# Two heads per attention step in the third block, and the delta-rule inverse in two 64-column tiles

## What is computed

```python
low = jnp.where(strict, jnp.einsum("bhnid,bhnjd->bhnij", kb, k) * decay, 0.0)
rhs = jnp.concatenate([v * beta, kb * jnp.exp(gc)[..., None]], axis=-1)
sol = lax.linalg.triangular_solve(low + jnp.eye(c, dtype=jnp.float32), rhs,
                                  left_side=True, lower=True, unit_diagonal=True)
```

```python
s = jnp.einsum('bhqd,bhkd->bhqk', qc, k) * scale
s = s + (cqc[..., None] - cum[:, :, None, :])
s = jnp.where(kpos[None, :] <= qpos[:, None], s, -jnp.inf)
p = jax.nn.softmax(s, axis=-1)
return jnp.einsum('bhqk,bhkd->bhqd', p, v)
```

## Time and profile before

| what | us |
|---|---|
| median of 3 runs (1081.12 to 1082.15) | 1081.33 |
| the profiled execution, its own time | 1081.43 |
| its span, first to last instruction | 1079.6 |
| PE busy | 1051.2 |
| DVE busy | 756.2 |
| ACT busy | 542.3 |
| PEld busy | 932.7 |

### The profile page before, as it was taken

How to read it: one execution, slowest core, us unless ns; L and a number is a source line. 1 busy time by engine, 2 the same in 40 slices (tenths; PEclk the granted TensorE clock), 3 DMA queues, 4 the chain that set the end, 5 groups by cost and what they waited for, 6 DMA issues and landing times.

```text
span 1079.6 us, 19214 instructions
## 1 busy us (share of the span) xinstructions
PE 1051.2 (97%) x7938; PEld 932.7 (86%) x7938; DVE 756.2 (70%) x1051; ACT 542.3 (50%) x601; POOL 12.6 (1%) x13
## 2 busy tenths in 40 slices
PE   9999999999999999999999999989999989999998
PEld 7999999999976798989899877659986659999986
DVE  6989947678458767677777856857797765556535
ACT  5675534563353463547536334576677654353331
POOL 0100000000000000000000000002000000000000
PEclk8999999999999999999999999999999999999999
DMA  8454432334325663425343354776344364545441
GB/s 343 157 180 155 157 118 90 138 125 159 115 79 213 252 239 155 132 104 193 121 157 118 118 200 153 310 291 260 127 156 156 103 243 163 195 172 181 176 163 51
DMA packets 26293, 181.32 MB, mean 168 GB/s; under 512 B 3040, under 2 KB 3296, under 8 KB 4960
## 3 DMA queue, kind: packets, MB, share of 16 engines
q1 hardware_dynamic: 25056, 174.66, 44.1%
q10 hardware_dynamic: 1152, 5.45, 1.2%
HBM read 179.04 MB, written 1.05 MB: 167 GB/s over the span
## 4 chain that ended last, share of the span: by engine, by line
PE 89%; DVE 7%; ACT 2%; issue 1%; DMA 1%; ACTq 0%; DVEq 0%; SPq 0%
PE PS L912 86%; DVE WL L1778 1%; PE PS L1065 1%; PE PS L1143 1%; DVE X L1972 1%; DVE X L1971 1%; DMA RAW<-wst 1%; PE PS L1289 0%; DVE layer_ln L2083 0%; DVE STAT L1953 0%; DVE X L1952 0%; ACT block L1606 0%; DVE X L2264 0%; DVE XTL L1995 0%; DVE layer L2076 0%
## 5 line engine op out<-in xcount | busy, mean ns | idle before, releaser
L912 PE MATMUL PS<-XTH,WH 128*128 128x256 f32 x1392 | 404.4, 291 | 0.7 <-issue 0.5
L912 PE MATMUL PS<-XTH,WL 128*128 128x256 f32 x1392 | 394.5, 283 | 0.0
L912 PE MATMUL PS<-XTL,WH 128*128 128x256 f32 x1392 | 394.4, 283 | 0.0
L1778 DVE TENSOR_TENSOR WL<-RAW,WH 128x2048 fp32r<-128x2048 f32 x138 | 316.9, 2297 | 107.9 <-ACT WH L1368 104.7
L1368 ACT ACTIVATE WH<-RAW 128x2048 fp32r<-128x2048 f32 x138 | 262.7, 1903 | 194.8 <-PE PS L912 191.2
L912 PEld LDWEIGHTS PS<-XTH,WH 128*128 128x128 f32 x1392 | 267.6, 192 | 6.3 <-issue 3.7
L912 PEld LDWEIGHTS PS<-XTL,WH 128*128 128x128 f32 x1392 | 267.7, 192 | 2.8 <-issue 2.6
L912 PEld LDWEIGHTS PS<-XTH,WL 128*128 128x128 f32 x1392 | 267.5, 192 | 0.0
L912 PE MATMUL PS<-WH,YH 128*128 128x512 f32 x224 | 89.6, 400 | 1.1 <-DVE YL L2256 1.1
L912 PE MATMUL PS<-WH,YL 128*128 128x512 f32 x224 | 87.4, 390 | 0.0
L912 PE MATMUL PS<-WL,YH 128*128 128x512 f32 x224 | 87.3, 390 | 0.0
(11 more groups left out here) (295 smaller groups left out, 1178.0 us busy)
## 6 DMA issues: line engine op xcount, KB each, us to landing
RAW<-wst SPq DMA_DIRECT2D x162, 1024.0 KB, 4.9
LNW<-lnrow ACTq DMA_DIRECT2D x3, 1024.0 KB, 6.4
RAW<-wst SPq DMA_DIRECT2D x4, 512.0 KB, 4.8
layer<-xt SPq DMA_DIRECT2D x2, 512.0 KB, 5.8
XR<-x ACTq DMA_DIRECT2D x1, 1024.0 KB, 6.2
out<-X SPq DMA_DIRECT2D x4, 256.0 KB, 2.1
CST<-cst ACTq DMA_DIRECT2D x1, 640.0 KB, 8.9
PT<-pt SPq DMA_DIRECT2D x1, 512.0 KB, 5.6
```

The lines of the kernel that those rows point to most:

```text
L912: return pe.matmul(o, lhsT, rhs, start=start, stop=stop)
L1778: tt(WL[:, i % RAW_RING, 0:n], RAW[:, i % RAW_RING, 0:n], as_float(WH[:, k % SPLIT_RING, 0:n]), ALU.subtract).then_inc(vector_done, 1)
```

## The change

The `gp` and `gu` matmuls of level 1 and above are each split in two, with 64 of the 128 weight columns and half of the output partitions each. Scores and value products of two heads become one PE step each (`scores:p`, `pvs:p`), in which the instructions of the two heads stand in turn. `scores:p` writes bank 0 and bank 1 and so claims both; it counts as read when DVE has done the odd head. `ORDER_T` is rewritten for the heads; `ORDER_V` and `ORDER_S` keep theirs but for `gm` ahead of `qn:1:1` ahead of `score:0` on DVE, and 14 ahead of 15.

```diff
@@ plan @@
         if n < HEADS:
-            step("score", n, on="TV" if FOX <= n < FOX + ML else "TVS", banks=(n % 2,), readers="V")
+            if n % 2 == 0:
+                step("scores", n // 2, on="T", banks=(0, 1), readers="V", read_in=("score", n + 1))
+            step("score", n, on="V" if FOX <= n < FOX + ML else "VS")
         if 1 <= n <= HEADS:
             step("turn", n - 1, on="TS", banks=(2,))
         if n >= 2:
-            if n % 2 == 0:
-                step("pv", n - 2, on="T", banks=(3,))
-            else:
-                step("pv", n - 2, on="TS" if FOX < n - 2 < FOX + ML else "TSV", banks=(3,), opens=False)
+            if n % 2:
+                ml = FOX < n - 2 < FOX + ML
+                step("pvs", n // 2 - 1, on="T", banks=(3,), readers="S" if ml else "SV", read_in=("pv", n - 2))
+                step("pv", n - 2, on="S" if ml else "SV")
@@ ORDER_T (one line of five) @@
-feat:4 first:feat:5 feat:5 grow:1 feat:6 first:feat:7 qn:1:0 feat:7 first:val:0:0 qn:1:1 score:0 val:0:0 first:val:0:1
+feat:4 first:feat:5 feat:5 grow:1 feat:6 first:feat:7 qn:1:0 feat:7 first:val:0:0 qn:1:1 scores:0 val:0:0 first:val:0:1 scores:1 turn:0 val:0:1 turn:1 first:val:1:0 scores:2 turn:2 pvs:0 turn:3
@@ ORDER_V @@
-split:94:114 feat:3 grow:0 split:96:116 feat:4 mod:1 grow:1 split:97:117 mb split:98:118 qn:1:0 gm score:0 qn:1:1
+split:94:114 feat:3 grow:0 split:96:116 feat:4 mod:1 grow:1 split:97:117 mb split:98:118 qn:1:0 gm qn:1:1 score:0
@@ t_gp, and t_gu alike with XI and PM @@
-                    last = mm(odd(PS[:, c, h * P:(h + 1) * P], i), DL[:, m, :], odd(U[:, m, :], i))
+                    for b in range(2):
+                        r = slice(b * HD, (b + 1) * HD)
+                        last = mm(odd(PS[r, c, h * P:(h + 1) * P], i), DL[:, m, r], odd(U[:, m, :], i))
@@ t_score becomes t_scores @@
-                o = PS[:, step.banks[0], :]
-                mm(o[:, 0:P], Q2[r:r + HD, q, 0:P], Q2[r:r + HD, k, 0:P])
-                mm(o[:, P:3 * P], Q2[r:r + HD, q, P:T], Q2[r:r + HD, k, :]).then_inc(tensor_done, 1)
+                for queries, o, keys in ((slice(0, P), slice(0, P), slice(0, P)), (slice(P, T), slice(P, 3 * P), slice(0, T))):
+                    for a in range(2):
+                        r = slice(a * HD, (a + 1) * HD)
+                        last = mm(PS[:, a, o], Q2[r, q, queries], Q2[r, k, keys])
+                last.then_inc(tensor_done, 1)
@@ t_pv becomes t_pvs @@
-                mm(o[:, 0:P], V2[:, 0, vcol:vcol + HD], pt[:, 0:P])
-                mm(o[:, P:T], V2[:, 0, vcol:vcol + HD], pt[:, P:2 * P], stop=False)
-                mm(o[:, P:T], V2[:, 1, vcol:vcol + HD], pt[:, 2 * P:3 * P], start=False).then_inc(tensor_done, 1)
+                for o, c, block in ((slice(0, P), 0, 0), (slice(P, T), 0, 1), (slice(P, T), 1, 2)):
+                    for h in (2 * p, 2 * p + 1):
+                        _, _, r, vcol, _ = head(h)
+                        last = mm(PS[r:r + HD, 3, o], V2[:, c, vcol:vcol + HD], PTT[:, h % 2, block * P:(block + 1) * P],
+                                  start=block < 2, stop=block != 1)
+                last.then_inc(tensor_done, 1)
@@ s_turn @@
-                    act.wait_ge(tensor_done, tensor_at("pv", h - 2))
+                    act.wait_ge(tensor_done, tensor_at("pvs", h // 2 - 1))
@@ v_score @@
-                dve.wait_ge(tensor_done, tensor_at("score", h))
+                dve.wait_ge(tensor_done, tensor_at("scores", h // 2))
```

More of the change, by code:

```diff
@@ L500 @@
 first:feat:1 gcol qn:0:0 feat:1 first:feat:2 qn:0:1 feat:2 first:feat:3 qn:0:2 feat:3 first:feat:4 grow:0 first:feat:6
-feat:4 first:feat:5 feat:5 grow:1 feat:6 first:feat:7 qn:1:0 feat:7 first:val:0:0 qn:1:1 score:0 val:0:0 first:val:0:1
[L502 to L505, removed]
+feat:4 first:feat:5 feat:5 grow:1 feat:6 first:feat:7 qn:1:0 feat:7 first:val:0:0 qn:1:1 scores:0 val:0:0 first:val:0:1 scores:1 turn:0 val:0:1 turn:1 first:val:1:0 scores:2 turn:2 pvs:0 turn:3
+val:1:0 scores:3 turn:4 pvs:1 first:val:1:1 turn:5 scores:4 turn:6 pvs:2 val:1:1 turn:7 scores:5 turn:8 pvs:3
+ada:5:0 turn:9 scores:6 turn:10 pvs:4 turn:11 mln ada:5:1 adat:4 scores:7 adat:5 turn:12 pvs:5 turn:13 out2:0:0
+turn:14 pvs:6 out2:1:0 turn:15 pvs:7 first:out2:0:1
 first:out2:1:1 out2:0:1 out2:1:1 ada:10:0 ada:10:1 xt:5:0 xt:5:3 xt:5:2 ada:11:0 xt:5:1 adat:10 ada:11:1 adat:11 ff:0
@@ L535 @@
 val:1:1 turn:6 pv:5 turn:7 score:10 turn:8 pv:7 turn:9 score:11 pv:9 turn:10 score:12 mln ada:5:1 turn:11 score:13
-turn:12 pv:11 turn:13 score:15 score:14 split:103:125 split:104:126 pv:13 turn:14 turn:15 pv:15 rms:1:0:0 rms:1:0:1
+turn:12 pv:11 turn:13 score:14 score:15 split:103:125 split:104:126 pv:13 turn:14 turn:15 pv:15 rms:1:0:0 rms:1:0:1
 rms:1:1:0 rms:1:1:1 split:105:131 split:106:132 ada:10:1 xt:5:2 xt:5:0 ada:11:1 xt:5:3 xt:5:1 split:107:133
@@ L571 @@
 gates:1 ga gb split:90:110 gd split:91:111 qn:1:2 gcol gsp qn:0:0 split:92:112 qn:0:1 split:93:113 qn:0:2 split:95:115
-split:94:114 feat:3 grow:0 split:96:116 feat:4 mod:1 grow:1 split:97:117 mb split:98:118 qn:1:0 gm score:0 qn:1:1
+split:94:114 feat:3 grow:0 split:96:116 feat:4 mod:1 grow:1 split:97:117 mb split:98:118 qn:1:0 gm qn:1:1 score:0
 ratio:0 split:99:119 score:1 score:2 ratio:1 split:100:120 ratio:2 score:3 score:4 ratio:3 split:101:123 ratio:4 pv:1
 score:5 score:6 ratio:5 ratio:6 score:7 pv:3 score:8 ratio:7 ratio:8 pv:5 score:9 score:10 ratio:9 ratio:10 score:11
-score:12 ratio:11 mlz ratio:12 score:13 mln ratio:13 pv:11 adat:4 split:102:124 score:15 score:14 adat:5 ratio:14
+score:12 ratio:11 mlz ratio:12 score:13 mln ratio:13 pv:11 adat:4 split:102:124 score:14 score:15 adat:5 ratio:14
 split:103:125 ratio:15 pv:13 split:104:126 pv:15 first:out2:0:1 first:out2:1:1 rmsb:1:0 out2:0:1 out2:1:1 rmsb:1:1
@@ L1058, in t_gu @@
                     m = c * HG + h
-                    last = mm(odd(PS[:, 2 + c, h * P:(h + 1) * P], i), XI[:, m, :], odd(PM[:, m, :], i))
+                    for b in range(2):
+                        r = slice(b * HD, (b + 1) * HD)
+                        last = mm(odd(PS[r, 2 + c, h * P:(h + 1) * P], i), XI[:, m, r], odd(PM[:, m, :], i))
                 last.then_inc(tensor_done, 1)
@@ L1273, in t_grow, with t_scores @@
                 last.then_inc(tensor_done, 1)
[L1275 to L1276 removed]
+            def t_scores(step, p):
+                q, k = head(2 * p)[:2]
                 for t in (q, k):
[L1278 removed]
+                    if FOX <= 2 * p < FOX + ML:
                         pe.wait_ge(scalar_done, scalar_at("feat", t // 2))
                     else:
[L1281 to L1284 removed]
+                        i = int(2 * p >= FOX)
+                        pe.wait_ge(vector_done, vector_at("qn", i, (t - (QT["bq"] if i else 0)) // 2))
+                for queries, o, keys in ((slice(0, P), slice(0, P), slice(0, P)), (slice(P, T), slice(P, 3 * P), slice(0, T))):
[3 more added lines that the diff above has]
+                last.then_inc(tensor_done, 1)
             def t_turn(step, h):
@@ L1290, in t_turn, with t_pvs @@
                 last.then_inc(tensor_done, 1)
[L1292 to L1297, removed]
-                mm(o[:, 0:P], V2[:, 0, vcol:vcol + HD], pt[:, 0:P])
-                mm(o[:, P:T], V2[:, 0, vcol:vcol + HD], pt[:, P:2 * P], stop=False)
-                mm(o[:, P:T], V2[:, 1, vcol:vcol + HD], pt[:, 2 * P:3 * P], start=False).then_inc(tensor_done, 1)
+            def t_pvs(step, p):
+                pe.wait_ge(scalar_done, scalar_at("turn", 2 * p + 1))
+                pe.wait_ge(scalar_done, scalar_at("val", 2 * p // 8, 1))
+                for o, c, block in ((slice(0, P), 0, 0), (slice(P, T), 0, 1), (slice(P, T), 1, 2)):
[4 more added lines that the diff above has]
+                last.then_inc(tensor_done, 1)
             def t_mln(step):
@@ L1326, in _ @@
                      "hr": t_hr, "gates": t_gates, "feat": t_feat, "val": t_val, "qn": t_qn, "gcol": t_gcol,
-                     "grow": t_grow, "score": t_score, "turn": t_turn, "pv": t_pv, "mln": t_mln, "out2": t_out2,
+                     "grow": t_grow, "scores": t_scores, "turn": t_turn, "pvs": t_pvs, "mln": t_mln, "out2": t_out2,
                      "ff": t_ff, "down": t_down}
@@ L2214, in v_score @@
                     dve.wait_ge(tensor_done, tensor_at("turn", h - 2))
-                b = PS[:, bank_of("score", h), 0:3 * P]
+                b = PS[:, h % 2, 0:3 * P]
                 s = SC[:, h % 2, :]
```

2 lines of the change are left out of this document (1 added, 1 removed).

## The result

The changed kernel takes 1103.74 us (median of 4 runs, 1097.06 to 1104.21) against 1081.34 us: ratio 1.0191, 95% interval 1.0152 to 1.0231. It is 22.4 us slower; the forecast was 1093 us, range 1086 to 1101. Its runs lie further apart than those of before, and the mean granted clock goes with the time: 0.98 in three runs of 1103.5 to 1104.2 us, 0.992 in the one of 1097.06 us. The profiled execution took 1103.51 us.

A forecast was written before the change was run, and what follows sets the result against it. PE's list sets the time, but in the heads a loop through DVE, ACT and PE. Sum: -9.0 + 4.8 + 8.5 + 5.4 - 2.3 + 2 + 2.5 = +11.9 us, so 1093 us, range 1086 to 1101.

The forecast's parts named there:

- the three claims: Waits by claims of banks that DVE still reads: at scores:0, at scores:1 to scores:6, and at mln and scores:7.
- Term A: GDN inverse: 64-column tiles save 11.3 us over 48 steps, 2.3 us come back as waits; -9.0 us.
- B: scores:0: PE waits for DVE's read of qn:1:1 in bank 1, with nothing else to do; +4.8 us (4 to 5.5).
- C: scores:1 to scores:6: each waits for DVE's read of the odd head, leaving holes in DVE's work; +8.5 us (4 to 12).
- Term D: mln and scores:7 wait for bank 0: about 2.1 us at mln, 3.3 us of PE work delayed; +5.4 us (3.5 to 8).
- The end: Behind scores:7: less PE work, -2.3 us; DVE and ACT late with adat:4 and out2's weight splits, +2 us (0 to 3).
- The clock: Two new stops of 4 to 5 us should each bring a fall to 1.2 GHz; +2.5 us (0 to 4).
- Rival 2: Clock stays low among the heads: about 4 more falls at 1.7 us plus 3 us of longer links; 1103 us, chance 0.07.

The follow-up runs named there:

- e3: The changed kernel with 53 extra matmuls that nothing reads, in thirteen places where PE waited; 1097.77 us, ratio 1.0147.
- e9: The changed kernel with qn:1:1 in bank 2 in place of bank 1, order and all else unchanged; 1098.71 us, ratio 1.0165.
- e1: The kernel before with the 64-column tiles of gp and gu alone, heads as before; 1074.86 us, ratio 0.9938.
- e4: The changed kernel with two value projections put ahead of scores:0 and a third ahead of scores:1; 1102.04 us, ratio 1.0170.

## Why the prediction missed

The direction, the three claims and their places were right; the sum was 10 us too small. In the profiled execution +22.0 us stand against +11.9. By the prediction's own terms:

- **Term A, -9.0.** Measured -7.85 at the first rows of HGRN2. The 0.52 us for a step behind another was right, and so were the 2.3 us of waits: the trace has twelve new ones of 0.11 to 0.22 us in the inverse and just behind it, 2.3 us together. What was left out is the transposing step beside tiled ones, 0.59 for 0.44: the change of form was charged to one side only. The prediction's estimate by the overhead in the Trainium skill ("TensorEngine Tiling (Array Packing)", Performance Considerations, Instruction Overhead) would have made a step 0.83 us; the rows show 0.52. It added the 60 cycles to the 64 columns. The section also says that a matmul of one column takes as long as one of 60, which speaks for a least time instead, and the 32 ns for each instruction fit that better.
- **Terms B and C, +4.8 and +8.5.** 13.3 together; 13.8 measured in e3, where the clock is up, and 15.7 in the changed kernel. The sum was right, the split was not: e9 shows that B is no loss of its own, since DVE, late by its own list, stops PE one pair later anyway. No rival held that.
- **Term D, +5.4.** 6.6 with the clock up. e3 adds 7.36, but its fall at 859 us lies in the last part of it, from scores:7 to turn:12, which takes 2.53 us there and 1.81 in e9, where the clock is 1.00:

```profile
858.05 0.93 PE L913 MATMUL PS<-block 64*128 64x128 f32 x8 [2.32 <-DVE YL L1804]
...
860.58 0.84 PE L1297 MATMUL PS<-CST,block 128*128 128x128 f32 x3
```

```profile
858.32 0.93 PE L913 MATMUL PS<-block 64*128 64x128 f32 x8 [1.61 <-DVE YL L1798]
...
860.13 0.49 PE L1297 MATMUL PS<-CST,block 128*128 128x128 f32 x3
```

From turn:11 to scores:7 e3 takes 9.16 us at full clock, and 9.16 + 1.81 - 4.34 (turn:11 to turn:12 before) = 6.6. One part was too small: mln starts 3.5 us later against turn:11 (from 0.96 ahead of it to 2.55 behind), where 2.1 was charged. The other 3.1 us agree with the 3.3 of the chain behind mln.
- **The end, -2.3 and +2.** -0.3 forecast, about +0.4 measured: e9, with no fall behind turn:12, adds 0.07 there, and the fall that before has in this part costs it some 0.4 (turn:15 to ff:1 takes 33.48 us in before and 33.10 in e1, which has none).
- **The clock, +2.5 (0 to 4): the step that failed.** It said that "the two new stops of 4 to 5 us should each bring such a fall". The changed kernel has seven more stretches at 1.2 GHz than before, and they cost about 8.9 us, what is left of 22.0 when the measured terms are taken off: 1.2 at 714 us, 1.9 up to turn:11, 1.7 up to turn:12, 4.1 behind. Only the one at 796 us comes with a stop of 4 to 5 us. Ahead of that at 840 us the waits are 1.70 and 1.12 us, ahead of that at 850 they are 0.92 and 1.34, and it begins inside the one of 2.00; ahead of that at 861 stand 2.00 and 1.92, and at 714 it is a wait of 1.96 us that was there before. The price for one fall was right (1.24 to 1.6 us on dense work), the number of them was not. The same stops that term C counts one by one were never counted for the clock.

Of the 10.1 us that the sum was too small, the clock makes 6.4, D 1.2, A 1.2, the end 0.7, and B and C 0.5.

Rival 2, given 0.07, said 1103 us by four more falls and 3 us of longer links. Its total is what came, for the most part by its cause, but only in part at its place: in the loop of the heads, up to turn:12, the slow matmuls cost 3.6 us, ahead of it and behind it 5.3. Its argument against itself, that the stretch has about the same instructions as before, is what misled. The Trainium skill, "TensorE: Matmul & The Clock Gate", A second HAM failure mode, describes a kernel in which short idle times between groups of matmuls make the clock swing between its two levels and cost throughput; this trace agrees, with waits of 0.7 to 2.5 us (and one of 4.74) and seven more slow stretches than before. The same page (HAM oscillation) takes half of the throttled time as the penalty; an estimate by it for the 30.7 us more here would be 15 us. The runs show about 9, since PE waits for DVE and ACT in part of it.

What the prediction named for the profile: `128*64` products, the idle of 4.7 us ahead of scores:0, 2.0 us ahead of mln, and turn:7 to turn:9 at 6.3 us for 4.5 (5.55 with the clock up, in e3) all came; the idle ahead of scores:7 was 1.92 us instead of 4, since mln, ada:5:1 and adat:4 ran at half clock in it (852.05 to 857.69, 5.6 us; some 3.1 before).

## What to carry to other kernels

Packing two heads into one step saved PE time that nobody was waiting for (two scores in a row already took no longer than one) and paid with a claim of two banks; before such a step, list for each bank who read it last and what that reader still has in front of it. A wait taken away shows its worth only at the next place where PE runs without stops: e9's 4.74 us were worth nothing up to turn:11, one bank number for mln 9.4 by the medians (7.4 between turn:11 and turn:12 in the trace). And count short waits together when you price the clock: where they gathered here, PE fell to 1.2 GHz also behind waits under 2 us, and paid in the dense part that followed. Executions of such a kernel can also lie several us apart, so take more of them before you compare two.

## What was unexpected of the hardware

- Extra matmuls that nothing reads, put into waits, brought back 6.0 us in the changed kernel, though each wait still ended with the same read or copy.
- The clock doesn't fall at the same places in every execution of the same instructions: behind one wait of 1.96 us it fell in five traces with the tiles and stayed up in four. Runs of one and the same kernel differed by up to 8.7 us (e4) where short waits gather, and by 1.1 us in e1.
- Two score steps side by side in the kernel before, each on half of the rows and into its own bank, took 0.86 us together, where one alone took 0.85; writing their instructions in turn gave 0.86 again.
